# Routing list of a mixture-of-experts layer: the token one-hots move from VectorE and ScalarE to GpSimd

## The reference

```
logits = hf @ router_w + router_b                 # 1024 tokens x 32 experts
top_v, top_i = lax.top_k(logits, 4)
gates = softmax(top_v)
order = argsort(top_i.reshape(-1))                # the tokens, sorted by expert
pos = pad_start[e_sorted] + (arange(n_slot) - starts[e_sorted])
buf_tok = zeros(buf_len).at[pos].set(tok_sorted)  # which token stands in which slot
xb = hf[idx]                                      # then, block by block of slots:
y = (clamped swiglu of xb @ w_gu[e] + b_gu[e]) @ w_down[e] + b_down[e]
out = x + zeros.at[buf_tok].add(y * buf_w)
```

## Time and profile before

| | |
|---|---|
| median of 3 runs | 2211.1 us (2205.86 to 2212.8) |
| the profiled execution, its own time | 2206.86 us |
| its span | 2205.0 us |
| busy: PE, DVE, ACT, POOL | 96%, 73%, 57%, 40% |
| granted clock of PE over the span | 0.972 |
| start of the list (`posr` ready) | 676.0 us |
| first matmul of the experts' loop | 701.6 us |

### The profile page before, as it was taken

One profiled execution on the slowest core, in us unless ns is written; L12 is line 12 of the kernel. 1 busy time (PEld: TensorE's weight loads), 2 busy tenths in 40 slices (PEclk: granted clock), 3 DMA queues, 4 the chain that ended last, 5 costly groups with the idle time before them and its releaser, 6 DMA issues.

```text
span 2205.0 us, 38933 instructions
## 1 busy us (share of the span) xinstructions
PE 2107.9 (96%) x11205; PEld 1816.7 (82%) x11206; DVE 1601.9 (73%) x2117; ACT 1259.5 (57%) x1586; POOL 886.9 (40%) x868
## 2 busy tenths in 40 slices
PE   6999999999996999999999999999999999999994
PEld 5877777765886999889998899998887898898992
DVE  4455662553337888898888978878989888988874
ACT  4254443545224666677666666666767666776662
POOL 2014772234433334445334442434454534444430
PEclk9999999899996999999999999999999999999996
DMA  4334445303245779899778987978999988998978
GB/s 143 103 91 114 135 124 161 105 1 109 105 180 167 256 261 344 294 383 370 264 256 296 370 275 262 342 257 290 387 381 374 372 268 284 377 372 279 320 251 284
DMA packets 292568, 551.65 MB, mean 250 GB/s; under 512 B 39656, under 2 KB 51909, under 8 KB 292516
## 3 DMA queue, kind: packets, MB, share of 16 engines
q1 hardware_dynamic: 268980, 489.97, 65.5%
q0 software_dynamic: 22384, 56.82, 6.9%
q10 hardware_dynamic: 1152, 4.19, 0.5%
HBM read 513.54 MB, written 48.33 MB: 255 GB/s over the span
## 4 chain that ended last, share of the span: by engine, by line
PE 74%; DVE 3%; issue 2%; DMA 2%; ACT 1%; DVEq 0%; SPq 0%; POOLq 0%; POOL 0%; ACTq 0%
PE banks L2538 17%; PE banks L208 11%; PE banks L210 11%; PE banks L209 11%; PE banks L2540 7%; PE banks L1917 3%; PE banks L2474 2%; PE banks L2473 2%; PE banks L1277 1%; DMA RAW<-in_expert_w_gate_up 1%; DVE VL L1256 1%; PE banks L2537 1%; PE banks L1903 1%; PE banks L1902 1%; PE banks L2478 1%
## 5 line engine op out<-in xcount | busy, mean ns | idle before, releaser
L1256 DVE TENSOR_TENSOR VL<-RAW,VH 128x2048 fp32r<-128x2048 f32 x389 | 881.9, 2287 | 27.9 <-ACT VH L1251 24.0
L1251 ACT ACTIVATE VH<-RAW 128x2048 fp32r<-128x2048 f32 x390 | 734.4, 1910 | 110.7 <-PE banks L210 75.9
L2538 PE MATMUL banks<-T,VH 128*128 128x384 f32 x1920 | 542.3, 357 | 2.0 <-DVE T L1297 1.8
L2540 PE MATMUL banks<-T,VL 128*128 128x192 f32 x1680 | 421.9, 251 | 0.0
L2538 PEld LDWEIGHTS banks<-T,VH 128*128 128x128 f32 x1920 | 345.7, 189 | 3.3 <-issue 2.4
L2540 PEld LDWEIGHTS banks<-T,VL 128*128 128x128 f32 x1680 | 321.5, 191 | 0.5
L2207 POOL DMA_INDIRECT dX<-yb,ycur x32 | 73.2, 2286 | 416.6 <-DVE yb L2365 399.4
L208 PE MATMUL banks<-VH,T 128*128 128x512 f32 x544 | 211.9, 389 | 0.0
L209 PE MATMUL banks<-VL,T 128*128 128x512 f32 x544 | 211.9, 389 | 0.0
L210 PE MATMUL banks<-VH,T 128*128 128x512 f32 x544 | 211.8, 389 | 0.0
L208 PE MATMUL banks<-VH,A 128*128 128x512 f32 x512 | 204.1, 399 | 3.9 <-DVE A L2345 2.7
(11 more groups left out here) (391 smaller groups left out, 4037.4 us busy)
## 6 DMA issues: line engine op xcount, KB each, us to landing
RAW<-in_expert_w_gate_up SPq DMA_DIRECT2D x528, 512.0 KB, 6.9
RAW<-in_expert_w_down SPq DMA_DIRECT2D x262, 512.0 KB, 7.0
RW<-in_w_in SPq DMA_DIRECT2D x24, 512.0 KB, 5.7
xin<-in_x SPq DMA_DIRECT2D x8, 512.0 KB, 9.9
MBC<-dM SPq DMA_DIRECT2D x8, 512.0 KB, 10.9
dQ<-parts SPq DMA_DIRECT2D x8, 512.0 KB, 3.0
dK<-parts SPq DMA_DIRECT2D x8, 512.0 KB, 3.0
WRAW<-in_w_out SPq DMA_DIRECT2D x8, 512.0 KB, 8.5
```

The lines of the kernel that those rows point to most:

```text
L1251: act.activation(VH[:, i, ks], RAW[:, i, ks], ACT.Copy).then_inc(s_hi, 1)
L1256: dve.tensor_tensor(VL[:, i, ks], RAW[:, i, ks], VH[:, i, ks].bitcast(f32), ALU.subtract).then_inc(s_w, 1)
L2538: last = pe.matmul(o[:, 0:2 * NW], VH[:, c % 3, k, col], T2[:, k], start=k == 0, stop=k == KT - 1)
L2540: pe.matmul(o[:, HI_ALL], VL[:, c % 3, k, col], T2[:, k, HI_ALL], start=False, stop=False)
```

## The change

POOL makes `tokR` directly: for each tile and pick one `tensor_scalar` of 128 x 64, which compares `iotaR` with the pick's column of `posr` and multiplies by the token's number, 32 instructions in all. `oneR` and its semaphore are gone, and so are the eight comparisons on DVE and the eight multiplications on ACT. DVE signals `s_places` when `posr` is written. POOL's new work stands behind its waits for the stores of the tokens (`s_st`, `s_sh`) and ahead of its wait for the indices.

```
@@ on_gpsimd, ahead of the first gather
                 pool.wait_ge(s_sh[i], 16 * HT)
+            pool.wait_ge(s_places, 1)
+            for t in range(TT):
+                if t >= 2:
+                    pool.wait_ge(s_list, t - 1)
+                for k in range(TOPK):
+                    n = t * TOPK + k
+                    last = pool.tensor_scalar(tokR[:, t % 2, k], iotaR[:], posr[:, n:n + 1], tokid[:, t:t + 1], ALU.is_equal, ALU.mult)
+                last.then_inc(s_tok_r, 1)
             pool.wait_ge(s_ix, 2)
@@ on_scalar
-            for t in range(TT):
-                act.wait_ge(s_one_r, t + 1)
-                if t >= 2:
-                    act.wait_ge(s_list, t - 1)
-                act.activation(tokR[:, t % 2], oneR[:, t % 2], ACT.Copy, scale=tokid[:, t:t + 1]).then_inc(s_tok_r, 1)
@@ on_vector
-            link(dve.scalar_tensor_tensor(out=posr[:], in0=posu[:], scalar=-float(UN), in1=posf[:], op0=ALU.mult, op1=ALU.add))
+            dve.scalar_tensor_tensor(out=posr[:], in0=posu[:], scalar=-float(UN), in1=posf[:], op0=ALU.mult, op1=ALU.add).then_inc(s_places, 1)
             for t in range(TT):
                 ks = slice(t * TOPK, (t + 1) * TOPK)
-                if t >= 2:
-                    dve.wait_ge(s_tok_r, t - 1)
-                dve.tensor_tensor(oneR[:, t % 2], bc(iotaR[:].unsqueeze(1), [P, TOPK, UN]), bc(posr[:, ks].unsqueeze(2), [P, TOPK, UN]), ALU.is_equal).then_inc(s_one_r, 1)
                 if t >= 2:
                     dve.wait_ge(s_list, t - 1)
                 dve.tensor_tensor(oneU[:, t % 2], bc(iotaU[:].unsqueeze(1), [P, TOPK, NUM]), bc(posu[:, ks].unsqueeze(2), [P, TOPK, NUM]), ALU.is_equal).then_inc(s_one_u, 1)
```

More of the change, by code:

```diff
@@ L1178, in layer_kernel @@
     r5w = Region(A_X + 64 * KB, 10 * KB)
-    oneR = r5w.take("oneR", [P, 2, TOPK, UN])
     tokR = r5w.take("tokR", [P, 2, TOPK, UN], f32r)
@@ L1320, in s5 @@
             return sem("s5_" + n)
-        s_it, s_on, s_sel, s_rank, s_one_r, s_tok_r, s_one_u, s_list, s_e = (s5(n) for n in ("iota", "ones", "sel", "rank", "one_r", "tok_r", "one_u", "list", "exp"))
+        s_places = s5("places")
+        s_it, s_on, s_sel, s_rank, s_tok_r, s_one_u, s_list, s_e = (s5(n) for n in ("iota", "ones", "sel", "rank", "tok_r", "one_u", "list", "exp"))
         s_m, s_tab, s_tb, s_ix, s_ixz = s5("m"), s5("tabs"), s5("tab_rows"), s5("idx"), s5("idx_zero")
```

## The result

The changed kernel takes 2223.7 us (median of 7 runs, 2216.5 to 2230.7) against 2211.1 us before (7 runs, 2205.9 to 2216.0). The ratio is 1.006 with a 95% interval of 1.0043 to 1.0078: it is slower, by 9.5 to 17 us. The forecast was 2215, at most 2222, and no measurable change.

The account below looks back on a forecast made before the run. The prediction took PE as the bound, busy 96% of the span, with nothing between router and experts' loop hidden. A loop start 4.5 us later on the 2211.1 us median gave 2215.6, rounded to 2215; range 2207 to 2222.

Parts of the forecast that it names:

- What bounds the list now, and that POOL would pace it: Token list before the experts' loop: PE's 0.97 us a tile paces it now; POOL would, at 1.36 us before hold-ups.
- The step of a POOL instruction: In the list, from one new POOL instruction to the next: 0.34 us, 32 of them making 10.9 us.
- the slow kind: POOL rows with one operation, 2.6 to 3.3 ns a column over 0.19 us, giving 0.38 us for 64 columns.
- outer bound: In the list, POOL's step at 0.56 us and 0.62 us a tile held up: loop about 13 us later.
- DVE against POOL: In the list, `oneU` reading two SBUF tensors holds POOL up 0.3 us a tile, 2.4 us in all.
- DVE's lead: DVE, waiting only for PE's sixth tile, leaves the list 3.8 us later, while the list ends 5.8 us later.
- The gathers: Behind the list: second gather lands 5.7 us after the splits, or 5.8 us later than now if held; 4.5 taken.
- measurably slower: Rival for the list: POOL pays for the second operation or loses every `oneU` in full; about +10 us, 2221; 20%.
- The fast rival: Rival for the list: POOL's two-operation instruction steps at 0.20 us; loop -0.4 to +2 us, 2211 to 2213; 27%.
- That the gain is at most 0.4 us: At the list's front, even a free POOL gains only `oneU` starting 0.34 us earlier, say 0.4 us.

Follow-up runs that it names:

- forms: A separate program that only copies x and times POOL instructions of the list's shapes, with DVE idle or streaming; the list's instruction took 578 ns with DVE idle.
- psum: The changed kernel with `iotaU` copied once to PSUM, so `oneU` has one SBUF and one PSUM input; ratio 1.0054 to the kernel before.
- gate_after: The changed kernel with DVE's first two weight splits held back until the first gather has landed; ratio 1.0042 to the kernel before.
- gate_before: The kernel before with DVE's first two weight splits held back until the first gather has landed; ratio 0.9982 to the kernel before.
- late_splits: The kernel before with DVE's first two weight splits held back until POOL signals behind issuing the second gather; ratio 0.9981 to the kernel before.

## Why the prediction was wrong

*What bounds the list now, and that POOL would pace it:* right. PE and DVE wait for POOL in every tile, and ACT's freed time is not used.

*The step of a POOL instruction:* this is the term that failed. I took 0.34 us from the nearest form and size; it is 0.56 (`forms`, `psum`). That is 32 x 0.22 = 7.0 us. Two things were wrong in it. The rows of the slow kind had one operation and one scalar each, and I let the second operation and the second scalar cost nothing; they cost 0.14 us. And I put a fixed part of 0.19 us under all forms because the min-and-max rows have it; the comparison's is 0.28. The value stood in the prediction as its outer bound, reasoned from a doubling, with the outcome that it implies (about +13 us) outside the range.

*DVE against POOL:* right in size. I took 0.3 us a tile, 2.4 us in all; the difference of the changed kernel and `psum` is 2.5. With the step of 0.56 us and all else as I had it, my own sum gives the last `tokR` 676.2 + 17.9 + 2.4 = 696.5, 12.8 us later than before, and 12.9 (20.59 less 7.68) were measured. The page "SBUF — State Buffer" of the Trainium skill, section "Who interferes with whom", says that whoever starts first has the pair; the streams in `forms` agree for POOL (1.91 us at the median instead of 0.58), but DVE lost only 0.5 us in 20.

*DVE's lead:* right. By the formula, with the last `tokR` as measured and a tile of 2.51 us, DVE leaves 9.2 us later; it was 9.6 (701.39 - 684.12 against 683.71 - 676.04). The splits end 10.2 us later.

*The gathers:* the second step that failed. I carried over 5.7 us from the splits' end to the landing; in the changed kernel it is 7.9 (711.24 to 719.16). The first gather was held through both splits, a case that I had priced and given half weight; but I had the loop wait for the second gather's landing even so, and now it waits for the first one's. Its instruction ends 1.23 us behind the splits' end, where that of the second ended 0.93 behind it before, and from there to the landing pass 6.69 us instead of 4.79, while SP's queue moves the whole 2.1 MB of weights (711 to 722 us: packets, MB, share of the 16 engines):

```profile
q1 hardware_dynamic: 1088, 2.10, 57.8%
```

What I had not seen is the other half. Before, PE had turned the first gather's eight blocks while the second was under way; now all twelve are turned in one go behind the landing, and from there to the first matmul pass 5.4 us instead of 3.0. The terms add up: 10.2 + 0.3 + 1.9 + 2.5 = 14.9 us. `gate_after` shows that the stretch behind the list is the splits' doing, by what they hold up and by the weights that they release: with the splits behind the gathers it is 5.8 us shorter.

*The rival "measurably slower"* is what happened: the step stood at its outer bound (0.56 us), the held-up time well inside (0.31 us a tile of 0.62), and the 12.6 us between the medians lie near the +13 that it gave. Its argument against itself, that the 256-column comparison would have to be a poor guide, was mistaken: the row was a good guide to one operation (918 ns alone, 931 at the least in the kernel before), but the kernel has another form. *The fast rival* falls: of the forms timed in `forms` only min and max is fast. *That the gain is at most 0.4 us* could not be tested, since POOL never was the faster one.

Open stays why `posr` is written 8.1 us later in the one trace than in the other. It lies ahead of all edits but the one copy in `psum`, and the variants lie between. PE's granted clock from 400 to 450 us is 0.86 in the one and 0.78 in the other, which goes the right way, but no run shows that it is the cause.

## What to carry to other kernels

Price a moved instruction by its exact form: operations, per-partition scalars and width each had a price of their own here, and the fixed part of 0.36 us was paid 32 times. When neither row has the second operation, the doubled price belongs inside the range, since the whole sum hangs on it.

An engine that is freed gains nothing unless it paced the work: DVE lost eight instructions and then waited 1.8 us a tile.

Look at who runs beside a gather issued from POOL. One wait that kept two DVE instructions away from two gathers, and with them the weights that they release, was worth about 4 us, and 5.5 with the tokens moved between the splits; the most that I had given this change was 0.4.

## What the runs showed of the hardware

A POOL instruction that reads SBUF beside a stream of DVE instructions with two SBUF inputs took 1.91 us at the median instead of 0.58, with one of the inputs in PSUM 0.58; DVE slowed by 3% (20.27 us against 19.76). POOL's min and max on 64 columns takes 240 ns, compare and multiply 428, with two per-partition scalars 578. An indirect DMA issued from POOL took 1.04 to 1.34 us with DVE's splits held back (`gate_after`, `gate_before`), and 3.03 to 5.01 when one or two splits ran beside it (`late_splits`, before, after). A semaphore increment that stands behind an indirect DMA on POOL released DVE before that DMA's instruction started (694.27 against 694.45 in `late_splits`).
